# All projections of a two-layer mixer with activations held and weights moving, tokens on partitions, and no loops

## The reference

```python
mod = jax.nn.silu(c) @ w_ada + b_ada             # 2048 x 6144 per layer
shift, scale, gate = jnp.split(mod, 3, axis=-1)
h = _rmsnorm(x, norm_pre) * (1.0 + scale[:, None, :]) + shift[:, None, :]
z = h @ w_in                                     # 2048 x 14336
gb, gcin, u, g_c, q, k, v, g_r = jnp.split(z, offs, axis=-1)
y_conv = gb * _causal_short_conv(gcin * u, conv_w) * jax.nn.silu(g_c)
q, k = _rope(q, positions), _rope(k, positions) * (RET_DK ** -0.5)
ret = _head_groupnorm(_retention_chunkwise(q, k, v), gn_gain)   # 8 heads
y_ret = ret * jax.nn.silu(g_r)
o = jnp.concatenate([y_conv, y_ret], axis=-1) @ w_out           # 4096 x 2048
x = x + gate[:, None, :] * _rmsnorm(o, norm_post)
```

## Time and profile before

| | us |
|---|---|
| median of 3 runs (lowest, highest) | 1824.88 (1821.68, 1826.28) |
| the profiled execution, its own time | 1823.35 |
| its span, first to last instruction | 1821.5 |
| PE busy | 1756.4 (96%) |
| DVE busy | 1194.6 (66%) |
| ACT busy | 813.3 (45%) |
| POOL busy | 84.2 (5%) |
| mean granted clock of TensorE | 0.988 of full speed |
| read from memory | 407.46 MB, 225 GB/s over the span |

### The profile page before, as it was taken

One profiled execution on the slowest core, in us unless ns is written; L12 is line 12 of the kernel. 1 busy time (PEld: TensorE's weight loads), 2 busy tenths in 40 slices (PEclk: granted clock), 3 DMA queues, 4 the chain that ended last, 5 costly groups with the idle time before them and its releaser, 6 DMA issues.

```text
span 1821.5 us, 28042 instructions
## 1 busy us (share of the span) xinstructions
PE 1756.4 (96%) x9855; PEld 1493.1 (82%) x9855; DVE 1194.6 (66%) x1526; ACT 813.3 (45%) x1054; POOL 84.2 (5%) x89
## 2 busy tenths in 40 slices
PE   5689999999999999999989999999999999999997
PEld 3358888888888888888877888788888888888886
DVE  1467887786878778864558566567566665765454
ACT  2234444444444544554445345444444444455443
POOL 5000000000000000000010000000000000000001
PEclk9899999999999999999999999999999999999998
DMA  9987786777768676855543666656565655565551
GB/s 341 376 306 282 256 283 231 265 257 248 271 237 283 232 278 235 299 189 185 187 137 117 230 204 218 205 187 236 183 226 194 223 196 204 200 224 185 186 184 47
DMA packets 223265, 411.01 MB, mean 226 GB/s; under 512 B 7168, under 2 KB 40496, under 8 KB 222896
## 3 DMA queue, kind: packets, MB, share of 16 engines
q1 hardware_dynamic: 223008, 409.46, 65.0%
q10 hardware_dynamic: 144, 0.13, 0.0%
HBM read 407.46 MB, written 2.10 MB: 225 GB/s over the span
## 4 chain that ended last, share of the span: by engine, by line
PE 89%; DVE 3%; issue 3%; DMA 2%; ACT 1%; SPq 1%; POOL 0%; DVEq 0%; ACTq 0%; POOLq 0%
PE Z L1009 47%; PE Z L1007 25%; PE Z L1026 3%; PE Z L1027 3%; PE Z L1028 3%; PE Z L1006 3%; DMA stage<-in_w_ada 1%; DVE w_lo L626 1%; DMA yr<-in_x 1%; PE SC L1144 1%; DMA stage<-in_w_in 0%; PE SC L1061 0%; ACT w_hi L434 0%; PE IN L1041 0%; PE SC L1119 0%
## 5 line engine op out<-in xcount | busy, mean ns | idle before, releaser
L1009 PE MATMUL Z<-H,w_hi 128*128 128x512 f32 x3392 | 1193.5, 395 | 0.0
L1007 PE MATMUL Z<-H,w_lo 128*128 128x256 f32 x3584 | 968.1, 279 | 1.7 <-DVE H L702 1.2
L626 DVE TENSOR_TENSOR w_lo<-stage,w_hi 128x1024 fp32r<-128x1024 f32 x576 | 695.2, 1232 | 372.8 <-ACT w_hi L434 324.2
L434 ACT CAST w_hi<-stage 128x1024 fp32r<-128x1024 f32 x576 | 591.9, 1051 | 600.3 <-PE Z L1009 455.2
L1009 PEld LDWEIGHTS Z<-H,w_hi 128*128 128x128 f32 x3392 | 637.0, 188 | 141.9
L1007 PEld LDWEIGHTS Z<-H,w_lo 128*128 128x128 f32 x3584 | 675.2, 188 | 24.5 <-issue 7.4
L647 DVE SCALAR_TENSOR_TENSOR acc<-stage,c_silu,acc 128x512 f32<-128x512 f32 x240 | 179.6, 748 | 7.4 <-DVE w_lo L626 2.1
L1009 PE MATMUL Z<-Y,w_hi 128*128 128x512 f32 x480 | 168.0, 394 | 0.0
L440 ACT COPY lo_sb<-Z 128x256 f32<-128x256 f32 x224 | 82.4, 372 | 188.5 <-PE Z L1009 145.3
L1007 PE MATMUL Z<-Y,w_lo 128*128 128x256 f32 x512 | 136.7, 277 | 0.0
L1026 PE MATMUL Z<-w_hi,H 128*128 128x512 f32 x256 | 102.5, 401 | 6.3 <-DVE bufA L665 5.9
(11 more groups left out here) (147 smaller groups left out, 874.0 us busy)
## 6 DMA issues: line engine op xcount, KB each, us to landing
stage<-in_w_in SPq DMA_DIRECT2D x192, 1024.0 KB, 5.3
stage<-in_w_ada SPq DMA_DIRECT2D x96, 1024.0 KB, 7.2
stage<-in_w_out SPq DMA_DIRECT2D x64, 1024.0 KB, 5.1
stage<-in_w_in SPq DMA_DIRECT2D x64, 512.0 KB, 5.6
dec<-decay SPq DMA_DIRECT2D x9, 256.0 KB, 5.2
yr<-in_x SPq DMA_DIRECT2D x2, 1024.0 KB, 11.4
out<-stage SPq DMA_DIRECT2D x8, 256.0 KB, 2.4
bufC<-in_positions ACTq DMA_DIRECT2D x1, 128.0 KB, 5.5
```

The costliest lines, as they stand in the source:

```text
L434: nc.scalar.copy(w_hi[:, 2 * parity + h, :, :], stage[:, slot, 2 * h:2 * h + 2, :]).then_inc(s_hi, 1)
L626: V.tensor_tensor(w_lo[:, 2 * parity + h, :, :], stage[:, slot, 2 * h:2 * h + 2, :], w_hi[:, 2 * parity + h, :, :].bitcast(F32), ALU.subtr ...
L1007: ins = T.matmul(Z[t][:, 0:S], wl, act[:, 0:S], start=False, stop=False)
L1009: ins = T.matmul(Z[t][:, :], wh, act, start=False, stop=stop)
```

## The change

**The form.** Every block now has v's form: for each 128 input channels and each 128 tokens, TensorE holds the activations' two parts in turn, and 512 columns of `w_hi` or `w_lo` move. The accumulators are two buffers of two banks each (Z[0] and Z[1], 256 tokens by 512 columns); block q uses Z[q % 2]. Both parts sum in one place, so the copies and adds of lines 440 and 665 are gone, as is the wait of a block for the block just before it.

**Tokens on partitions.** The convolution and the transposed products still want channels on partitions. So per turn PE transposes four things of eight 128x128 pieces each (`turned`): q and k, the normalised heads, C times u, and the gate. Before, it was the heads alone. RoPE works along the free axis. The row sums of squares come out of ACT's `Square` with `accum_out`, 1/rms is a number per partition, and x is kept by tokens.

**The first turn, K-outer.** The first 28 chunks are taken group by group of input channels: four times the seven blocks. The partial sums lie in SBUF (`part`). Only the first 8 modulation chunks come ahead of the first weights; the other 24 lie two by two behind the first four chunks of each group. The side steps of turn 0 then run beside turn 1 (`FIRST`).

**The other modulation chunks.** 32 are summed on DVE in eight bundles of four neighbouring chunks (`ADA_SUM`) in turns 1 to 3 of layer 0, and 32 (the gates) in bundles of four at the head of each output block of both layers. None is left in layer 1's turns.

**Between the layers** there are neither spreading products nor matmuls without use; PE multiplies x by the diagonal of 1/rms (`x_columns`), which transposes and scales in one, 8 float32 products of 128 columns for each quarter of the channels.

**Unrolled.** There are no hardware loops; each engine's program is one straight piece.

The diff is a rewrite of the whole file; this is its core:

```diff
-                steps = order(TILES, kc == nk - 1)
-                for t, a in steps:
-                    if start:
-                        T.matmul(Z[t][:, :], wh, act, start=True, stop=False)
-                    ins = T.matmul(Z[t][:, 0:S], wl, act[:, 0:S], start=False, stop=False)
-                    if not start:
-                        ins = T.matmul(Z[t][:, :], wh, act, start=False, stop=stop)
+            def half_chunk(n, h):
+                ch = CH[n]
+                z = Z[ch.q % 2]
...
+                pe.wait_ge(s_lo, 2 * n + h + 1)
+                for i in range(NT):
+                    for a in (2 * h, 2 * h + 1):
...
+                        T.matmul(z[:, i, :], hh, wh, start=ch.first and a == 0, stop=False)
+                        T.matmul(z[:, i, :], hh, wl, start=False, stop=False)
+                        ins = T.matmul(z[:, i, :], hl, wh, start=False, stop=stop)
+                ins.then_inc(s_pe, 1)
+            def turned(dst, src):
+                for e in range(4):
+                    for i in range(NT):
+                        ins = T.transpose(dst[:, e, i * P:(i + 1) * P], src[:, i, e * P:(e + 1) * P], I)
+            def x_columns(l, g):
+                for t in range(4):
+                    for i in range(NT):
+                        k = 4 * g + t
+                        ins = T.matmul(four(xt_bank(l, g))[:, t, i * P:(i + 1) * P], xt[:, i, k * P:(k + 1) * P],
+                                       diag[:, i, :], start=True, stop=True)
+def chunk_table():
+    table, q = [], 0
+    for g in range(GROUPS):
+        for b in range(BLOCKS):
+            table.append(Chunk(False, 0, 0, b, g, q, True, True))
+            q += 1
...
+USUAL = Steps_at(rope=5, radd=6, trq=6, qkt=8, v=9, scores=7, p=9, inner=9, stats=11, sgr=13, yn=13, mult=14,
+                 tr=14, yrhi=16, yrlo=17, gcopy=17, cu=21, trc=21, y0=23, conv=24, sg=25, gate=29, trg=29,
+                 ymul=31, yhi=32, ylo=33)
+ADA_SUM = [base(t) + s for t, s in ((1, 20), (1, 26), (2, 5), (2, 12), (2, 20), (3, 5), (3, 12), (3, 20))]
+GATE_FROM, GATE_SUM, GATE_AT = 0, 5, 7
...
+            V.tensor_scalar(var2[:, :], xsq[:, :, 0], 1.0 / D, EPS, ALU.mult, ALU.add).then_inc(s_var, 1)
+            dve.wait_ge(s_pow, 1)
+            diagonals()
+            front_row(0)
...
+            def layer_end(l):
+                gated(l, NB - 1)
+                variance(ssq[:, :, :], 2 * l + 2)
+                for i in range(NT):
+                    for piece in range(2):
+                        V.scalar_tensor_tensor(xt[:, i, cols], og[:, i, cols], rs2[:, i:i + 1], xt[:, i, cols],
+                                               ALU.mult, ALU.add).then_inc(s_xn, 1)
-                with nc.Fori(1 if l == 0 else 0, TURNS, engines=(mybir.EngineType.PE,), hint_back_edge=True) as j:
-                    turn(l, j)
-                keep_clock(CLOCK_X)
-                x_sum(l + 1)
```

More of the change, by code:

```diff
@@ L18 @@
 import math
+from collections import namedtuple
 from contextlib import ExitStack
@@ L98, in mod_points @@
-def mod_points(layer):
-    return (GC, GB, GR) if layer == 0 else (GR,)
+BLOCK_COL = {VV: COL_V, GR: COL_GR, GC: COL_GC, UU: COL_U, GG: COL_G, GB: COL_GB}
+OUT_ORDER = (0, 1, 2, 4, 5, 6, 7, 3)
+PRM_B, PRM_PRE, PRM_GN, PRM_C, PRM_CW = 0, 96, 128, 160, 176
+PRM = 272
+Chunk = namedtuple("Chunk", "out l j b g q first last")
+def chunk_table():
[4 more added lines that the diff above has]
+            q += 1
+    for l in range(LAYERS):
+        for j in range(1 if l == 0 else 0, TURNS):
+            for b in range(BLOCKS):
+                for g in range(GROUPS):
+                    table.append(Chunk(False, l, j, b, g, q, g == 0, g == GROUPS - 1))
+                q += 1
+        for nb in range(NB):
+            for w in range(OUT_CH):
+                table.append(Chunk(True, l, nb, 0, w, q, w == 0, w == OUT_CH - 1))
+            q += 1
+    return table
@@ new lines, with base, steps @@
+FIRST = Steps_at(rope=2, radd=3, trq=4, qkt=6, v=3, scores=6, p=8, inner=9, stats=11, sgr=7, yn=13, mult=13,
+                 tr=17, yrhi=19, yrlo=20, gcopy=99, cu=8, trc=9, y0=11, conv=12, sg=9, gate=10, trg=21,
+                 ymul=23, yhi=24, ylo=25)
+ALL_TURNS = LAYERS * TURNS
+def base(t):
+    return AT_IN[0, 0, 0, GROUPS - 1] if t == 0 else AT_IN[t // TURNS, t % TURNS, 0, 0]
+def steps(t):
+    return FIRST if t == 0 else USUAL
+ADA = [(part, g) for g in range(GROUPS) for part in (1, 0)]
@@ new lines, with load_table, front @@
+ADA_SUM = [base(t) + s for t, s in ((1, 20), (1, 26), (2, 5), (2, 12), (2, 20), (3, 5), (3, 12), (3, 20))]
+GATE_FROM, GATE_SUM, GATE_AT = 0, 5, 7
+def load_table():
+    table = []
+    def front(g, part, kc):
+        table.append(("front", 2 * g + (1 - part), kc))
+    for part in (1, 0):
+        for kc in range(GROUPS):
+            front(0, part, kc)
+    for n, c in enumerate(CH):
+        for m, at in enumerate(ADA_SUM):
+            if at - GROUPS <= n < at:
+                table.append(("ada", m, n - at + GROUPS))
+        if c.out and GATE_FROM <= c.g < GATE_FROM + GROUPS:
+            table.append(("gate", NB * c.l + c.j, c.g - GATE_FROM))
+        table.append(("w", n, 0))
+        if n < FRONT and c.g < GROUPS - 1 and c.b < 4:
+            for i in range(2):
+                at = 2 * c.b + i
+                front(c.g + 1, 1 - at // GROUPS, at % GROUPS)
+    return table
@@ L103, in build, with stage_values @@
+LOADS = load_table()
+PLACE = {what: i for i, what in enumerate(LOADS)}
+def stage_values():
+    at, out = [0] * SLOTS, []
+    for i, (kind, n, _) in enumerate(LOADS):
+        at[i % SLOTS] += 32 if kind == "w" and not CH[n].out and CH[n].b == QK else 16
+        out.append(at[i % SLOTS])
+    return out
+STAGED = stage_values()
 def build(nc, x, c, positions, norm_pre, norm_post, w_ada, b_ada, w_in, conv_w, gn_gain, w_out,
@@ L314, in _, with gate_bank, tmp_buf @@
+        def gate_bank(t):
+            return four(B if t == 0 else A)
+        def tmp_buf(g):
+            return (R1, R3)[g % 2]
         @block.sync
         def _(sp):
[L316 to L323 removed]
@@ new lines, in variance, with diagonals @@
+            def variance(src, k):
+                me.then(V.tensor_reduce(var2[:, :], src, mybir.AxisListType.X, ALU.add))
+                me.wait()
+                V.tensor_scalar(var2[:, :], var2[:, :], 1.0 / D, EPS, ALU.mult, ALU.add).then_inc(s_var, 1)
+                dve.wait_ge(s_pow, k)
+            def diagonals():
+                for i in range(NT):
+                    ins = V.tensor_scalar(diag[:, i, :], ident[:, 0:P], rs2[:, i:i + 1], None, ALU.mult)
+                ins.then_inc(s_diag, 1)
@@ new lines, in front_chunk @@
+            def front_chunk(k, kc):
+                i = PLACE["front", k, kc]
+                pe.wait_ge(s_stage[i % SLOTS], STAGED[i])
+                if kc == 0 and k >= 2:
+                    pe.wait_ge(s_mod, k - 1)
+                for a in range(CK):
+                    ins = T.matmul(A[COL * a:COL * (a + 1), k % 2, :], c_cols[:, CK * kc + a, :],
+                                   stage[:, i % SLOTS, a, :], start=kc == 0, stop=kc == GROUPS - 1)
+                ins.then_inc(s_front, 1)
@@ L1198, in _ @@
[L1198 to L1209 removed]
+                            p = p_buf(t)
```

1597 lines of the change are left out of this document (716 added, 881 removed).

## The result

The changed kernel takes 1785.07 us in the median (1783.31 to 1787.98, 4 runs), the kernel before 1825.26 us (1821.68 to 1826.28). The ratio is 0.9777, with a 95% interval of 0.9759 to 0.9795. The forecast was 1794 us, with 1780 to 1806 as its own range.

A forecast was written before the change was run, and what follows sets the result against it. PE's stream was taken to bound 1504 of 1821.5 us. Stage changes -8.0 + 3.8 + 3.7 - 8.2 - 10.8 - 10.6 = -30.1 us on 1823.35 gave 1793.2, stated as 1794 us, range 1780 to 1806.

The forecast's parts named there:

- Form: All 256 weight chunks: moving instead of held weights, 5.44 us a chunk against 5.54, saving 0.10 each, 26 us in all.
- Loops: Back edges at turn starts: 4.2 us of each looped turn are not work and go when unrolled.
- the forecast of layer 1's turns: Layer 1's turns: 609.3 us of chunks, 28.6 side work, 4.9 x columns; 642.8 us, a change of -10.8.
- Transposes: Side work of the turns: 24 more transposes a turn, eight per 0.87 us, adding 21 us on PE.
- rival 4: Transposes on PE cost their 272 ns duration each, adding 31 us, for 1825 us; chance 0.03.
- Bundles, layer 0: Layer 0's turns: PE waits for late weights beside eight modulation bundles, 6 us in all; stage +3.8 us.
- Bundles, outputs: Two output stages: gate sums 3.3 us and bundle waits 2 us each, 179.4 us each, together +3.7.
- Rival 2, the starved ring: Layer 0's turns 1 to 3 and output blocks: late ring slots cost PE 3.4 to 4 us a bundle, 1840-1850 us; chance 0.10.
- Rival 3, better ends: Shorter POOL steps, no late loads: front 245 us, seam 17, bundles nothing, 1770 us in all; chance 0.17.
- Front: First 28 chunks: POOL's angles take 26 us, first weight chunk at 58 us, stretch 259 us, -8 us.
- Seam and tail: Between the layers 19.5 us, -8.2; at the end 12.5 us, -10.6, with 4.3 for the last store.
- The forecast's closing sentence: End of the sum: of 26 us from the form, 21 go to transposes; what stays comes from ends, seam and loops.

The follow-up runs named there:

- the run with loops and form: Kernel before, all loops unrolled and every block's matmuls in the moving form, projections' values not computed: 1782.91 us, ratio 0.9755.
- The loops alone: Kernel before with every hardware loop written out on every engine, nothing else changed: 1815.77 us, ratio 0.9929.
- The slower gate chunks: Changed kernel with two more DVE passes over the accumulator in each of 32 gate chunks: 1799.15 us, ratio 0.9852.
- the version with the power first: Changed kernel with POOL's first power ahead of the angles and ACT's two sines after the eleventh chunk's cast: 1774.15 us, ratio 0.9699.

## Why the prediction was right, and where its terms were not

**Form.** Right in kind: 0.227 us between starts in every block. Wrong in size: 0.10 us a chunk was read from one stretch of 25 held pairs, which was among the fast ones. The mean over all held matmuls gives 0.14 a chunk, and 36 us instead of 26, as the run with loops and form shows (33 by the medians, 35.5 by the spans). One stretch is not the mean of a form.

**Loops.** 4.2 us of a turn were found as the rest of 164.4, the longest of three, after pricing its chunks with that same low rate. The loops alone gave 2.1 to 2.8; of the 1.4 above 160.2 that stay in a turn without them, 1.0 is the form (24 x 0.04). Neither error reaches the forecast of layer 1's turns (642.8, measured 642.6), because that stretch was built from the moving form's own rate and not by subtraction. Only the way the gain was divided was wrong.

**Transposes.** 21 us forecast, 19 measured; 109 ns for one was met where they were doubled in a stretch without waits, and rival 4 falls. The Trainium skill's figure for one (TensorE: Matmul & The Clock Gate, Part 4: PE-mode transpose), about 275 ns, is again met by the 272 ns of duration and not by the 109 ns that a doubled one added.

**Bundles, layer 0.** The term "6 us over the eight bundles" was too large. PE's waits there show 1.9 us at a single place (at 403 us) and no more, and the stage came out at -0.8 where +3.8 was forecast. The wait that is there is of the kind foreseen: the load starts at 392.48 us, behind a fourth pass that ended at 392.04, lands at 400.91, and then the convolution's eight taps (3.33 us of DVE, until 404.04) stand before the subtraction. At the other bundles the lead covered the delay.

**Bundles, outputs.** Forecast +3.7 us, measured +7.7. A gate sum makes its own chunk and the next 0.46 and 0.45 us longer, 3.6 us a stage (3.3 forecast). Eight transposes of the last turn fall in each stage (0.8, which the forecast had in the turns). The rest, 3.5 and 2.3 us, is the bundles (2 each forecast). The mechanism was right: the forecast's "the next load of such a pair waits for the sum of the modulation chunk two before" is what the waits show, and four of the six late starts in the output stages are at the fifth chunk of a block, by 0.45 to 0.9 us, where "about 0.4 us late" was said.

**Rival 2, the starved ring.** Its loop exists, and at its size: from 795.07 us, where the pair of loads starts behind the fourth pass, to 810.04, where the next one does, pass 15.0 us for two chunks (14.9 forecast). But it costs PE at most 2 us at any bundle, not 3.4 to 4. PE's stock of ready weights covers the rest: at a block's first gate chunk the fourth pass ends within 1 us of PE's start of that chunk, and only from the third on up to 4.1 us behind it. The slower gate chunks show the other way into it: once DVE's own 5.33 us are made longer than PE's 5.44, the excess is handed on almost one for one in the gate chunks behind the first.

**Rival 3, better ends,** had the seam (17 us, measured 16.7) and was close for the bundles of layer 0's turns; at the front the time came between the two (254 us, where the forecast had 259 and the rival 245).

**Front.** Its first chunk was to come at 58 us and came at 50.1. The step that failed is "I take 26 us" for POOL's steps. The timeline of POOL after has

```profile
14.61 0.53 POOL L889 TENSOR_SCALAR R<-R 128x128 f32<-128x128 f32 x1
```

where the 256 columns took 0.85, so a step has a smaller fixed part than the power's 0.73 us for two elements had suggested: that is another operation. The angles ended at 31.7 us, not 39.6; the chain behind them took the 18.4 us that were forecast. From the first chunk to the 28th the forecast had 201 us; it took 204.0, with 18.4 instead of 15.5 us above the content of 185.6. That moved the whole front by 4.9 us.

**Seam and tail.** Chains of single durations held well: four updates in 4.87 (5.2 forecast), x columns at half clock 3.65 (3.3). The seam came out 2.8 us shorter than 19.5: from the end of the first x columns to the first chunk passed 2.5 us, where I had 4.9, because (by the same timelines) the second x columns lie wholly beside h and the first chunk waits for the first half of h's split only. The tail, from DVE's and SP's timelines:

```profile
1773.28 4.87 DVE L691 SCALAR_TENSOR_TENSOR xt<-og,rs,xt 128x1024 f32<-128x1024 f32 x4 [0.84 <-POOL rs L873]
1774.59 3.92 SPq L438 DMA_DIRECT2D out<-xt  x4
```

Each quarter's store is issued as soon as it is updated, so only the last is left behind the fourth, and 4.3 us for it was too much by about 1.

So the sign came from the right places and the stages' sum was built rightly, from the stream at 0.227 us and the two ends. Of the 10 us by which the time fell below the forecast's, 4.9 are the front and 4.2 the seam and the tail; layer 0's turns (4.6) are made up for by the outputs (4.0), which is luck. The forecast's closing sentence, that form and transposes nearly cancel (26 against 21) and the rest brings the gain, does not hold: the form is worth 33 to 36 us against 19. The kernel before with its loops written out and the moving form, and nothing else of the change, already has the span 1778.3 (the changed kernel 1781.5), though without the transposes that the form asks for. So what the change adds to those two, transposes, bundles and sums against the shorter seam and ends, comes out about even.

## What to carry to other kernels

Build the stretch after from rows of the new form and don't read the gain of an edit as the rest of a subtraction: two wrong parts can hide in one right whole. Where side work shares a ring with the main stream, follow the slot round: when the side work gives it back, how long the next load then takes, and what still has to happen to the data. Compare that with what the main engine needs for the same chunks. Here the helper had time to spare on its own account; moving half of its passes earlier was worth some 9 us, and spreading its chunks out cost as much. And when an order is rewritten, look at what the first product waits for: a 0.7 us power behind 18 us of angles that nobody needed yet cost 10 us.

## What the runs showed of the hardware

- The pair of held matmuls (512 and 256 columns) takes 0.3465 us in most blocks and 0.353 in some, at full clock, while 24 matmuls of the moving form take 5.44 us in every block that has neither side work nor a wait.
- After 34 busy matmuls and 2.8 us idle, the granted clock was 0.80 and 0.58 in the two stretches in which PE worked again; without them, after 10.5 us idle, it was 0.51 and then 1.00 in the changed kernel, 0.50 and 0.70 in the version with the power first.
- A gate sum, one float32 product of 128x512 that the trace shows as two instructions, lengthens the stream by 0.91 us, 0.46 in its own chunk and 0.45 in the next.
- A 1 MB load of weights landed 5.2 us after its start as the first of two started together (at 810.04 us of the changed kernel) and 8.0 us after it as the second of two (at 795.48).
- POOL's step on 128 columns takes 0.53 us, on 256 it took 0.85.
